# A two-layer hybrid encoder step: input projection in 512-column chunks on five banks, and in 256-column chunks on three

## The reference

```
xn  = rmsnorm(x)
q, k, v, qi, ki, wi, u, gv = xn @ w_in        # 512, 128, 128, 256, 32, 8, 512, 512 columns
score = sum_h relu(qi_h . ki) * wi_h          # 8 index heads of 32, over all keys
keep the top 128 keys of each row (48 for the sample rows)
a   = softmax(q . k over the kept keys) v     # 8 heads of 64, 2 KV heads
b   = gelu(u) * (w_spatial @ rmsnorm(gelu(gv)) + bias)
x  += [a, b] @ w_out
x  += relu(rmsnorm(x) @ w_ff1)^2 @ w_ff2
```

## Time and profile before

| what | us |
|---|---|
| median of 3 runs (lowest, highest) | 1421.72 (1419.63, 1423.68) |
| the profiled execution, its own time | 1423.89 |
| its span, first to last instruction | 1421.6 |
| TensorE busy (share of the span) | 1360.3 (96%) |
| VectorE busy | 711.7 (50%) |
| ScalarE busy | 516.2 (36%) |
| GpSimd busy | 219.8 (15%) |
| share of the chain that ended last: L1576 / L1312 | 65% / 13% |

### The profile page before, as it was taken

One profiled execution on the slowest core, in us unless ns is written; L12 is line 12 of the kernel. 1 busy time (PEld: TensorE's weight loads), 2 busy tenths in 40 slices (PEclk: granted clock), 3 DMA queues, 4 the chain that ended last, 5 costly groups with the idle time before them and its releaser, 6 DMA issues.

```text
span 1421.6 us, 21711 instructions
## 1 busy us (share of the span) xinstructions
PE 1360.3 (96%) x9033; PEld 1239.4 (87%) x9033; DVE 711.7 (50%) x1298; ACT 516.2 (36%) x906; POOL 219.8 (15%) x239
## 2 busy tenths in 40 slices
PE   6999798999999999999999997989999999999997
PEld 5766575999999999999986675679999999999997
DVE  4387843445434444444636886425544444343453
ACT  5355644333223123133324664434321322322322
POOL 4234254110000000000211535322000000000011
PEclk8999898999999999999999999989999999999999
DMA  5211111232232323222331111104233232323221
GB/s 176 60 45 31 30 45 30 70 88 84 81 88 77 89 75 89 82 82 75 95 101 46 45 30 30 30 17 126 75 89 84 81 89 75 89 76 89 75 75 68
DMA packets 169763, 102.34 MB, mean 72 GB/s; under 512 B 7433, under 2 KB 159937, under 8 KB 169665
## 3 DMA queue, kind: packets, MB, share of 16 engines
q1 hardware_dynamic: 169664, 100.95, 24.5%
HBM read 96.98 MB, written 3.95 MB: 71 GB/s over the span
## 4 chain that ended last, share of the span: by engine, by line
PE 89%; DVE 4%; issue 3%; ACT 2%; POOL 2%; DMA 1%; SPq 0%; DVEq 0%; ACTq 0%; POOLq 0%
PE bank L1576 65%; PE bank L1312 13%; PE bank L1426 3%; PE bank L1474 2%; PE bank L1451 2%; DVE late L1025 1%; PE bank L1332 1%; DVE m L1023 1%; DMA late<-in_x_prompt 1%; PE bank L1377 1%; DVE late L1056 1%; PE bank L1496 1%; PE bank L1618 1%; PE bank L1351 0%; POOL late L550 0%
## 5 line engine op out<-in xcount | busy, mean ns | idle before, releaser
L639 ACT ACTIVATE ring_hi<-ring_raw 128x1024 fp32r<-128x1024 f32 x176 | 184.8, 1050 | 276.1 <-PE bank L1576 248.7
L1576 PE MATMUL bank<-vh,ring_hi 128*128 128x288 f32 x1280 | 276.9, 298 | 2.8 <-DVE vl L1124 2.8
L1576 PE MATMUL bank<-vh,ring_lo 128*128 128x288 f32 x1280 | 276.6, 298 | 0.0
L1576 PE MATMUL bank<-vl,ring_hi 128*128 128x288 f32 x1280 | 276.3, 297 | 0.0
L923 DVE TENSOR_TENSOR ring_lo<-ring_raw,ring_hi 128x1024 fp32r<-128x1024 f32 x162 | 211.2, 1304 | 94.6 <-ACT ring_hi L639 87.6
L1576 PE MATMUL bank<-xh,ring_hi 128*128 128x288 f32 x1024 | 220.8, 297 | 1.9 <-issue 1.9
L1576 PE MATMUL bank<-xl,ring_hi 128*128 128x288 f32 x1024 | 220.3, 296 | 0.0
L1576 PE MATMUL bank<-xh,ring_lo 128*128 128x288 f32 x1024 | 220.2, 296 | 0.0
L1576 PEld LDWEIGHTS bank<-vh,ring_hi 128*128 128x128 f32 x1280 | 206.6, 190 | 3.7 <-DVE vl L1124 3.7
L1576 PEld LDWEIGHTS bank<-vh,ring_lo 128*128 128x128 f32 x1280 | 206.5, 190 | 0.0
L1576 PEld LDWEIGHTS bank<-vl,ring_hi 128*128 128x128 f32 x1280 | 206.4, 190 | 0.0
(11 more groups left out here) (194 smaller groups left out, 1538.3 us busy)
## 6 DMA issues: line engine op xcount, KB each, us to landing
ring_raw<-in_w_ff SPq DMA_DIRECT2D x128, 512.0 KB, 4.0
ring_raw<-in_w_in SPq DMA_DIRECT2D x32, 512.0 KB, 3.7
ring_raw<-in_w_out SPq DMA_DIRECT2D x32, 128.0 KB, 2.9
ring_raw<-in_w_out SPq DMA_DIRECT2D x16, 256.0 KB, 3.1
late<-in_x_prompt SPq DMA_DIRECT2D x4, 512.0 KB, 6.6
out_y_prompt<-late SPq DMA_DIRECT2D x4, 512.0 KB, 3.9
w_sp<-in_w_spatial SPq DMA_DIRECT2D x2, 512.0 KB, 4.5
gate_bc<-in_gate_norm SPq DMA_DIRECT2D x2, 256.0 KB, 5.4
```

The costliest lines, as they stand in the source:

```text
L639: s.activation(ring_hi[:, n % NSLOT, :], ring_raw[:, n % NRAW, :], ACT.Copy).then_inc(hi_ready, 1)
L1576: last = mm(bank[unit_bank(u) + half][:, 0:HALF], w[:, k, :], a[:, k, HALVES[half]], start=k == 0 and w is wh and a is ah, stop=k == KT - ...
```

## The change

The projection's chunks are 256 columns wide (index queries; K and V; then Q, GV, U in two halves each): eight chunks, each in two halves of the contraction over five tiles, again 80 slots a layer, of twelve matmuls of 256 columns. The tiles of a chunk are interleaved by `ORDER`, and from the second chunk on they rotate over three banks (0, 1, 2). That frees banks 3 and 4: index products go four heads at a time on four strips and banks 3 to 6, score steps take both KV heads at a time on two strips and banks 3 and 4. VectorE multiplies and adds the index scores of all four tiles (`NXV` = 4 x 8), GpSimd none. GpSimd takes the low parts of ring blocks 6 to 18 of a layer (before 12 to 18). ScalarE evacuates each 256-column sum into SBUF a slot after its end, GELU of the gate and of U becomes an instruction of its own over the whole row (U: from slot 76). The tables are new; transposes come five slots after the scores and products with V two slots after the transposes. In layer 0 all copies of x come first, then two splits, then the squares; `row_sums` stands behind slot 6. VectorE does the index rope of tiles 2 and 3.

```diff
-    CW = 512
-    CHUNKS = [C_K, C_Q, C_GV, C_U]
+    CW = 256
+    QI, KV, Q0, Q1, GV0, GV1, U0, U1 = range(8)
+    CHUNKS = [C_K + 2 * DKV, C_K, C_Q, C_Q + CW, C_GV, C_GV + CW, C_U, C_U + CW]
...
-    NXV = 3 * NIH
-    TR_AT = {22: [0, 1], 23: [2, 3], 27: [4], 29: [5], 31: [6], 33: [7]}
-    PAIR_AT = {g: p for p, g in enumerate([*range(25, 37), 37, 39, 41, 43])}
-    SCORED = dict(zip(INDEX_TILES, [29, 33, 37, 48]))
-    QT_AT = {41 + a: a for a in range(NT)}
-    QK_AT = [*range(45, 55), *range(59, 67), *range(70, 78)]
-    GV_EVAC = {57: [0, 1, 2], 58: [3], 59: [4]}
-    GV_SQUARE = {58: [0, 1], 59: [2, 3], 60: [4]}
-    U_EVAC = {NG_IN: [0, 1], NG_IN + 1: [2], NG_IN + 2: [3], NG_IN + 3: [4]}
-    FILL = [(0, 0), (29, 2), (33, 3), (37, 4), (45, 2), (55, 4), (59, 2), (67, 4), (70, 0)]
+    NXV = 4 * NIH
+    ORDER = [(0, 0), (1, 0), (0, 1), (1, 1), (2, 0), (3, 0), (SMP, 0), (2, 1), (3, 1), (SMP, 1)]
+    def proj_bank(c, t):
+        return t if c == 0 else (NT * (c - 1) + t) % 3
+    SUMS_AT, SMALL_AT, TURN_AT = 6, 7, 9
+    TR_AT = {14: [0, 1], 15: [2, 3], 24: [4], 26: [5], 28: [6], 31: [7]}
+    QUAD_AT = {17: 0, 19: 1, 21: 2, 23: 3, 25: 4, 27: 5, 30: 6, 33: 7}
+    SCORED = dict(zip(INDEX_TILES, [21, 25, 29, 35]))
+    QT_AT = {38: 0, 39: 1, 43: 2, 44: 3, 45: 4}
+    QK_AT = [41, 43, 45, 47, 49, 54, 56, 58, 60, 67, 69, 71, 73]
+        T_AT[max([QK_AT[LAST_QK[g]] + 5, *(x + 1 for x in T_AT)])] = k
+    GELU_AT = {61: [0, 1, 2], 62: [3, 4]}
+    SQUARE_AT = {61: [0, 1], 62: [2, 3, 4]}
+    U_GELU_AT = 76
+    FILL = [(0, 0), (21, 2), (34, 3), (41, 2), (50, 3), (67, 0)]
...
-        POOL_SPLITS = range(S_OUT - 4, S_OUT + NSLOT)
+        POOL_SPLITS = range(6, S_OUT + NSLOT)
...
+            for j in range(KT):
+                s.activation(xh[:, j, :], x[:, j, :], ACT.Copy, scale=gain(0, j)).then_inc(xh_ready, 1)
+            split_hi(1)
+            split_hi(2)
+            for j in range(KT):
+                feed(j, 0)
...
+                        elif k0 == 0:
+                            prior = NT * c + t - (NT if c == 1 and t < 3 else 3)
+                            pe.wait_ge(proj_evac, NT * NC * l + prior + 1)
+                        for kx in range(k0, k0 + nk):
+                            for a_, w_ in ((xh, w[0]), (xh, w[1]), (xl, w[0])):
+                                last = mm(bank[b][0:ROWS[t], 0:CW], a_[:, kx, cols(t)], w_[:, kx % KH, :],
...
                     for a, k in ((qih, kh), (qih, kl), (qil, kh)):
-                        for m in (i, i + 1):
+                        for j in range(4):
+                            b = ID * j
+                            last = mm(bank[3 + j][0:rows, 0:KEYS[t]], a[b:b + ID, blk, cols(t)], k[b:b + ID, 0:KEYS[t]],
...
+                    for e in range(h):
                         for m, kk in ((q_hi, kh), (q_hi, kl), (q_lo, kh)):
+                            for kv in range(NKV):
+                                b, blk = HD * kv, ITEMS[FIRST[k] + e][1]
+                                last = mm(bank[3 + kv][0:ROWS[t], e * S:(e + 1) * S], m[b:b + HD, blk, cols(t)],
```

More of the change, by code:

```diff
@@ new lines, in hybrid_encoder_program, with half_sums, ended @@
+    NP = HALFS * NT
+    NG_IN = NP * NC
+    ORDER = [(0, 0), (1, 0), (0, 1), (1, 1), (2, 0), (3, 0), (SMP, 0), (2, 1), (3, 1), (SMP, 1)]
+    def half_sums(s):
+        c, o = divmod(s, NP)
+        if c == 0:
+            if o >= NT:
+                return [(o - NT, KH, KH)]
+            return [(m % NT, KH // 2 * (m // NT), KH // 2) for m in (2 * o, 2 * o + 1)]
+        t, half = ORDER[o]
+        return [(t, KH * half, KH)]
+    def ended(c, t):
+        return NT + t if c == 0 else NP * c + ORDER.index((t, 1))
@@ new lines, in proj_bank, with free_at @@
+    def proj_bank(c, t):
+        return t if c == 0 else (NT * (c - 1) + t) % 3
+    def free_at(c):
+        return NP * c + (NT - 1 if c == 0 else ORDER.index((SMP, 0)))
+    HI_AT = {free_at(c) + 1: HALFS * c + 3 for c in range(NC)}
+    HI_AT.update({NP * c: HALFS * c + 2 for c in range(1, NC + 1)})
+    SUMS_AT, SMALL_AT, TURN_AT = 6, 7, 9
+    ROOT0_AT = 7
+    EVAC = {}
+    for c in range(NC):
+        for t in range(NT):
+            EVAC.setdefault(9 if (c, t) < (0, SMP) else ended(c, t) + 1, []).append((c, t))
@@ L133, in cols @@
+    MEAN_AT, ROOT_AT = 64, 65
+    SCALE_AT = {66: [0, 1], 67: [2, 3, 4]}
+    GAIN_AT = {67: [0, 1], 68: [2, 3, 4]}
+    MIX_AT = {70: 0, 71: 1, 72: 2, 73: 3, 74: 4}
+    MIX_BANK = [5, 6, 5, 6, 7]
+    U_GELU_AT = 76
+    MT_BANK = [4, 2, 3, 0, 1]
+    T_BANK = [5 + k % 2 for k in range(NS)]
+    FILL = [(0, 0), (21, 2), (34, 3), (41, 2), (50, 3), (67, 0)]
     def cols(t):
@@ L947, in _ @@
             dve.wait_ge(g_ready, 1)
-            for n in range(KT // 2):
-                if n < NSLOT:
-                    split_lo(n)
-                feed(2 * n, 0, 0)
-                feed(2 * n + 1, 0, 0)
+            split_lo(0)
+            for j in range(KT):
+                feed(j, 0, 0)
+            split_lo(1)
+            split_lo(2)
             for l in range(DEPTH):
@@ L1162, in _ @@
                         topk_next(at)
-                    if t == 1 and QUARTERS <= n < S_OUT and n + NSLOT - 1 not in POOL_SPLITS:
-                        split_lo(N0 + n + NSLOT - 1)
+                    if at - 1 in T_AT:
+                        p_low(T_AT[at - 1])
+                    if at - 1 in QK_IN:
+                        k = QK_IN[at - 1]
+                        tile = TILE_ORDER[QK[k][0]]
+                        if QK[k][1] == 0 and tile:
+                            while done[tile] < total_steps(tile):
+                                topk_next(at)
+                            dve.wait_ge(dve_step, step_of[tile])
+                        for i in step_items(k):
+                            masked_logits(i)
                     for i in TR_AT.get(at, ()):
```

593 lines of the change are left out of this document (295 added, 298 removed).

## The result

The changed kernel takes 1428.4 us (1426.3 to 1430.5, 5 runs) against 1421.7 (5 runs) before: ratio 1.004, 95% interval 1.0024 to 1.0055. It is **slower by 0.4%**; the forecast was 1403, faster by 1.3%. The profiled execution has a span of 1426.6 us, 5.0 more than before.

What follows compares the result with a forecast made beforehand. TensorE bounds the attention stretches, except a VectorE stall ending II and ScalarE and VectorE in the tail. Terms -3.4, -9, +0.6 make -11.8 us a layer, -23.6 for two, +5 in layer 0: 1421.7 to 1403 us, range 1382 to 1432.

Steps and rivals of the forecast that it cites:

- the sum of II: Slots 21 to 56 of a layer: TensorE busy 84, wait at slot 56 8, other pauses 3: 95 us, -9.
- the burst: Slot 55: 21 top-k steps of 0.56 us run in one slot (11.8 us), so TensorE waits 8 us.
- It stays at 88.5 - 2.3 = 86 us: VectorE's busy time in slots 21 to 56: ring splits -6.8, top-k steps -2.2, weighted adds +6.7.
- rival 2: GpSimd's splits hold up VectorE's weighted adds between slots 18 and 34, up to 9.6 us; 1413 us, chance 0.13.
- Small waits: TensorE's remaining pauses in slots 21 to 56: 3 us; many small waits eating the gain, chance 0.08.
- Layer 0's start: Row sums behind slot 6 wait 4 us for squares and adds, then about one at the lower clock: +5 us.
- overlap fully: Index products: two strips in two banks run at once, six products in 0.89 us, not 1.40; quads give -4 us.
- Rival 3: K=64 score pairs or index quads go one after another; 11.2 + 4 us a layer come back; 1427 us, chance 0.07.
- rival 1: Slot 55's top-k steps are hidden and ScalarE keeps up: 12.4 us a layer go; 1378 us, chance 0.12.
- The stall at slot 64: Slots 61 to 64: ScalarE's GELUs, squares and exps make a transposed block's split late; TensorE stalls 4.4 us.
- III: Slots 57 to 79 and the tail: TensorE busy 67.5, stall 4.4, tail waits 4: 76 us, +0.6.
- rival 4: Projection chunk starts wait for banks ScalarE must evacuate, 2 us at each of 14 in two layers; 1431 us, chance 0.20.

Runs made afterwards that it cites:

- a2: Changed kernel, GpSimd's low parts of ring blocks 6 to 11 done for 64 of 1024 columns only (output wrong): 1408.0 us.
- d3: Kernel before the change, with only the low-part splits of ring blocks 6 to 11 moved to GpSimd: 1429.6 us.
- a4: Changed kernel with half the top-k steps (64 and 24 keys kept, so another output): 1406.4 us.
- a1: Changed kernel with tile 3's top-k steps begun in slot 55 instead of 35: 1404.5 us.
- d2: Changed kernel with a1, a2 and a3 together: 1381.6 us.
- b4: b3 with VectorE doing a slot's top-k steps behind everything else of that slot instead of ahead: 1401.1 us.
- d1: c1 with c4's top-k order and rate (40 steps done by slot 40 instead of 47): 1390.8 us.
- a3: Changed kernel with the small columns' products ahead of the row sums, and their weights' rounding in layer 0 between the squares: 1419.8 us.
- d4: Changed kernel with all index quads and score steps on the array's first strip (another output): 1444.4 us.
- b2: Changed kernel with the products of an index quad or score step ordered strip by strip: 1427.4 us.
- b1: Changed kernel with the low-part splits of ring blocks 6 to 11 back on VectorE: 1420.4 us.
- c1: Changed kernel with a1, a3 and b1 together: 1385.8 us.
- b3: Changed kernel with a3, tile 3's top-k steps from slot 55, SMP's and tile 2's from slot 36: 1397.1 us.
- c4: Changed kernel with a1, a3, blocks 7 and 8 split on VectorE, top-k steps by due time (2 a slot to slot 40, then 3): 1389.0 us.

## Why the prediction was wrong

**The step that failed** is the sum of II, "84 + 8 + 3 = 95", in its last term, "I leave 3 of the rest". TensorE's busy time (84.5) and the wait behind the burst (8.2) came out. The other pauses were 15.2 us instead of 3: one wait of 6.1 at slot 41, which the forecast does not have, and 9.1 of short ones. The wait at slot 41 was left out because of the step before, "It stays at 88.5 - 2.3 = 86 us" together with "Because the adds come in quads with air between them I don't count it in the sum". VectorE measured 96.4. Two things were mis-sized in it:

- *The stretching of VectorE's work beside GpSimd* (rival 2, given 0.13) was there: 7.2 us a layer (96.4 against a2's 89.2). Its price as a rival, up to 9.6, was right; that only half the gain would go was not. It lay wholly ahead of slot 41, where VectorE had no air: 34.9 of 38.2 us. The forecast had four splits of GpSimd between slots 18 and 34; three run there, but five before what slot 41 waits for. a2 takes the held instructions away and leaves VectorE's list as it is, and gives 20.4 us. d3 moves the same splits in the kernel before; single adds are held there too (one for 2.57 us), and it costs 7.3. The sign given for this rival, "weighted adds above 1.5 us", is in the profile: 2.57 and 2.70 us. Who reads only the means of the groups (0.94 and 1.06) misses it. The Trainium skill ("SBUF — State Buffer", Who interferes with whom) says that a VectorE instruction with two SBUF inputs contends with a GpSimd instruction that reads SBUF, and one with at most one input, outside the two-port modes, does not. The trace agrees on both: the adds go from 0.76 to 1.06 us on average, `max` stays at 0.68.
- *The top-k steps.* The forecast counted 100 in slots 21 to 56, four fewer than before; 109 lie there, five more. Its hand count passed over slot 44, where tile 1 is finished with six steps instead of two, so that at the burst's end as many are done as before (104 in both traces). The other five, all of 512 keys, VectorE does behind the burst, before TensorE comes to slot 57. Together that is 3.7 us more than before where the forecast had 2.2 less. Against these 13.1 the sum had other terms too high by 2.7, more than half of it because four instructions of 256 keys moved into slots 0 to 20 with their quads.

**Why 10 us of VectorE became 13 of time.** The forecast compared VectorE's 86 us with a stretch of 95 and saw 9 to spare. But the queue is in order: TensorE ran nearly unhindered to slot 41 and waited there for an instruction at the end of VectorE's backlog. a4 shows this best: with 23 us less on VectorE in the stretch, the wait at slot 41 grew. It cost 6.1 us, and with the lower clock behind it the slot took 10.5. The other half of the 13 are the short waits.

**The burst** was right in place and size (8 forecast, 8.2 measured), but dearer than its wait: a1 gains 23.9 us, 8.8 in layer 1's slots 21 to 56 and 13 in layer 0's. In slots 50 to 56 alone TensorE's pauses fall from 13.3 to 3.9 us in both layers.

**Small waits** were set at 3 us in II. With burst and stretching gone (d2) the stretch takes 91.9 us with 82.8 busy: 9.1 of waits and pauses. That is the second mis-sized term. The 3 came from the kernel before, whose pauses in II were nearly all the burst and one wait for the same low part of the queries, there behind ScalarE:

```profile
PE bank L1403 <- DVE vl L1101: 3.0, 1, 3.0
```

The changed kernel has score steps, transposes and products with V in other slots, and the waits between them are new. Which chain makes them stays open; b4 excludes the order of VectorE's queue within a slot, d1 that fewer steps ahead of slot 41 would remove them.

**Layer 0's start** was forecast at 5 us. The wait was 6.4 for 4, and a3, which removes it, gains 8.6. Slots 6 to 20 are 9.3 us shorter in a3, 2.9 more than the wait: behind it the ten products of the row sums alone took 1.1 us longer than in layer 1, at a granted clock of 0.50. The lower clock held on longer than the one microsecond given.

**Right** were the terms of TensorE: projection 1.44 us a slot (slots 0 to 20 39.2 for 39.6), quads from 12.1 to 5.8 us (-6.3 for -4), scores from 24.7 to 14.4 (-10.3 for -11.2), busy time in II 84.5 for 84. One reading behind them was too strong: two strips do not "overlap fully" when six products take 0.89 us instead of 1.40, that is 1.6 times and not 2; a quad of twelve took the same 0.91, so the index products fell by half and more. Rival 3 (strips do not overlap) is excluded by d4, rival 1 (burst hidden) by the wait of 8.2. The stall at slot 64 (4.6 for 4.4) was right; the tail is 12.0 us where 8 to 10 were given, and the whole of III 76.6 for 76. Of rival 4 (three banks) there is no wait at a chunk's start in the profile: slots 34 to 40 take 10.9 us, 1.55 each. Its number, 1431, was near the result, for another reason.

In sum: slots 21 to 56 took 12.9 us more than forecast in layer 1 and 13.2 in layer 0 (109.3 for 96.0), layer 0's slots 0 to 20 took 2.9 more (50.1 for 47.3), and the other parts of the two stretches 1.0 more. Layer 0's first product starts 3.1 us earlier (16.8 for 19.9, but 19.5 in b2, which starts alike, so that is luck). What lies behind the stretches is 3.2 shorter: the first 10 us behind each ran at a granted clock of 1.00, before at 0.83. That makes 23.7 of the 23.6 us between -18.6 and +5.0.

## What to carry to other kernels

Take the second engine's load not over a stretch but up to each instruction that the bound engine waits for; work queued ahead of it counts in full, however much air comes after. Before moving work to GpSimd, look at what VectorE does at that moment: two-input instructions beside the moved work are held until it is over, and here that cost VectorE as much as it freed (b1). A filler loop that takes turns between an urgent tile and a later one doubles the burst when the urgent one falls due; beginning the later one only when the urgent one is done was the largest single gain (a1), and with two more edits it turns this change into -2.5% (c1). Ordering all steps strictly by due time (b3, c4, d1) gave little or nothing beyond that.

## What the runs showed that was not expected

- Strips overlap whatever the order of the products is: a quad of 12 products of 512 columns takes 0.98 us with the strips alternating and 0.98 with them one after another (b2). On one strip the index products of a layer take 16.7 us (d4), in pairs 12.1, in quads 5.8: 2.9 times.
- Single instructions with one tensor input are held as well: a `TENSOR_SCALAR` of 512 keys takes 0.49 us in a2 and 1.32 beside GpSimd's rope steps, one of 192 keys 0.23 in a2 and 1.52 beside a GpSimd split.
- A stall can cost more than its length, by the lower clock behind it: 6.4 us of waiting and 9.3 of time at layer 0's start (a3), 6.1 and 9.8 at slot 41 in layer 1 (8.2 in layer 0; a2). At the burst it is less clear: with 9.4 us less of pauses in slots 50 to 56 in each layer, a1 gains 8.9 us there in layer 1 and 11.9 in layer 0. The same slots with the same waits differ by up to 2.7 us between executions (layer 0's slots 21 to 56: 109.3 in the changed kernel, 106.6 in b2), so a factor is not to be had from one pair.
